# Extra output tiles between the steps of six norm chains, and weights split six units ahead instead of four

## What is computed

```
h = [meta; x]
h = h + mixer(rms_norm(h))          # differential attention (4 heads x 2) and windowed attention (8 heads), gated, merged
h = h + swiglu(rms_norm(h))         # 1024 -> 2816 -> 1024
x = rms_norm(h)
for layer in 0, 1:
    m = mixer_a(rms_norm(x)) if layer == 0 else mixer_c(rms_norm(x))
    # mixer_a: short convolution and latent attention (8 heads)
    # mixer_c: compressed, selected and windowed attention (16 heads, 4 groups), gated
    x = x + rms_norm(m)
    x = x + rms_norm(sq_relu_mlp(rms_norm(x)))     # 1024 -> 4096 -> 1024
```

## Time and profile before

| what | us |
|---|---|
| median of 3 runs | 2252.34 (2251.35 to 2252.68) |
| the profiled execution: its own time | 2250.42 |
| its span | 2248.6 |
| PE busy | 2086.2 (93%) |
| DVE busy | 1210.6 (54%) |
| ACT busy | 808.4 (36%) |
| POOL busy | 38.3 (2%) |
| mean granted clock of PE | 0.957 |

### The profile page before, as it was taken

How to read it: one execution, slowest core, us unless ns; L and a number is a source line. 1 busy time by engine, 2 the same in 40 slices (tenths; PEclk the granted TensorE clock), 3 DMA queues, 4 the chain that set the end, 5 groups by cost and what they waited for, 6 DMA issues and landing times. The chain is left out here.

```text
span 2248.6 us, 27344 instructions
## 1 busy us (share of the span) xinstructions
PE 2086.2 (93%) x10625; PEld 1011.3 (45%) x10625; DVE 1210.6 (54%) x2191; ACT 808.4 (36%) x1481; POOL 38.3 (2%) x40
## 2 busy tenths in 40 slices
PE   6978899999999988988889999979979998999996
PEld 2443454444444433435434444437446653444442
DVE  4875545546555346665376632356665536765332
ACT  3345543323233222345233321234357743332220
POOL 0100000000000002000000000000000000000000
PEclk9989999999999999989989999987989999999998
DMA  5310013324333322311213333306300011433310
GB/s 180 113 48 0 1 38 102 99 69 124 104 96 113 99 67 85 104 40 64 75 57 114 102 103 113 113 30 207 94 10 1 1 36 40 122 103 113 113 57 38
DMA packets 52185, 179.18 MB, mean 80 GB/s; under 512 B 5985, under 2 KB 9697, under 8 KB 51681
## 3 DMA queue, kind: packets, MB, share of 16 engines
q1 hardware_dynamic: 52064, 177.51, 25.7%
HBM read 174.34 MB, written 2.10 MB: 78 GB/s over the span
## 5 line engine op out<-in xcount | busy, mean ns | idle before, releaser
L1491 DVE SCALAR_TENSOR_TENSOR w_lo<-w_raw,w_hi 128x1024 f16<-128x1024 f32 x317 | 382.0, 1223 | 238.5 <-ACT w_hi L1161 238.2
L815 PE MATMUL pS<-xx,w_hi 128*128 128x512 f16 x1264 | 484.3, 383 | 19.3 <-DVE tmp L1546 14.3
L816 PE MATMUL pS<-xx,w_hi 128*128 128x512 f16 x1264 | 484.1, 383 | 0.0
L817 PE MATMUL pS<-xx,w_lo 128*128 128x512 f16 x1264 | 483.8, 383 | 0.0
L815 PE MATMUL pS<-arena,w_hi 128*128 128x512 f16 x924 | 350.7, 380 | 1.4 <-DVE arena L1506 1.4
L816 PE MATMUL pS<-arena,w_hi 128*128 128x512 f16 x924 | 350.6, 379 | 0.0
L817 PE MATMUL pS<-arena,w_lo 128*128 128x512 f16 x924 | 350.5, 379 | 0.0
L1161 ACT ACTIVATE w_hi<-w_raw 128x1024 f16<-128x1024 f32 x317 | 322.9, 1042 | 21.6 <-PE pS L838 20.9
L1170 ACT ACTIVATE arena<-src 128x512 f16<-128x512 f32 x106 | 66.7, 630 | 377.8 <-DVE src L2046 202.5
L815 PEld LDWEIGHTS pS<-xx,w_hi 128*128 128x128 f16 x1264 | 124.7, 99 | 171.5 <-DVE tmp L1546 18.3
L817 PEld LDWEIGHTS pS<-xx,w_lo 128*128 128x128 f16 x1264 | 124.7, 99 | 152.6 <-issue 6.1
(11 more groups left out here) (299 smaller groups left out, 2331.3 us busy)
## 6 DMA issues: line engine op xcount, KB each, us to landing
w_raw<-in_w SPq DMA_DIRECT2D x317, 512.0 KB, 3.6
X<-in_x SPq DMA_DIRECT2D x1, 2112.0 KB, 8.6
arena<-in_c SPq DMA_DIRECT2D x2, 1024.0 KB, 6.8
out_t<-X SPq DMA_DIRECT2D x8, 256.0 KB, 2.0
arena<-in_h SPq DMA_DIRECT2D x4, 256.0 KB, 15.0
arena<-in_h SPq DMA_DIRECT2D x2, 512.0 KB, 9.2
arena<-in_c SPq DMA_DIRECT2D x2, 256.0 KB, 4.0
arena<-arena SPq DMA_DIRECT2D x4, 128.0 KB, 2.6
```

Of the source, the lines that this page charges most:

```text
L815: pe.matmul(ps, wh, ah, start=f, stop=False)
L816: pe.matmul(ps, wh, al, start=False, stop=False)
L817: mm = pe.matmul(ps, wl, ah, start=False, stop=l)
L1491: dve.scalar_tensor_tensor(out=w_lo[:, u % WR, :], in0=w_raw[:, u % RAW, :], scalar=WS, in1=w_hi[:, u % WR, :], op0=ALU.mult, op1=ALU.subt ...
```

## The change

- `Plan` keeps two lists: `bank` (0 to 3 are `pS`, 4 is `pT[:, 0]`, 5 is `pO[:, 0]`) and `before` (the tile that had the bank last). For the stages in `SPARE` two tiles, from the number given on, get banks 4 and 5; all others take `pS`'s four in turn.
- `lead` puts the sums behind all slices, then one such tile, then the spread, then the second one. For qa's lead these are qb's tiles 0 and 1, for kvc's lead ks's, for the others the stage's own tiles 4 and 5.
- In the first block qb comes ahead of ka, on every engine and in the stream; PE waits for the eviction of qb's first two tiles ahead of ka. qb's first two units are split ahead of the norm.
- `LOOK` is 6 instead of 4. On SP three weight units go between the krp and the qrp copies.
- `ck1`'s and `cv1`'s bias columns move to `pO[:, 1]` and `pT[:, 1]`.

```diff
-LOOK = 4
+LOOK = 6
 ...
+SPARE = {"ffgu": 4, "cv": 4, "up0": 4, "up1": 4, "ks": 0, "qb": 0}
 ...
+        self.bank, self.before = [], []
+        turn, last = 0, {}
+        for s in self.order:
+            for j in range(s.n):
+                extra = j - SPARE.get(s.name, s.n)
+                b = 4 + extra if 0 <= extra < 2 else turn % 4
+                turn += b < 4
+                self.before.append(last.get(b, -1))
+                self.bank.append(b)
+                last[b] = s.o0 + j
 ...
-    [("qa", "T", 4, KD, 1), ("ka", "T", 4, KD, 1), ("va", "N", NQ, KD, 4), ("qb", "T", 4, KD, 1),
+    [("qa", "T", 4, KD, 1), ("qb", "T", 4, KD, 1), ("ka", "T", 4, KD, 1), ("va", "N", NQ, KD, 4),
 ...
+        def out_bank(o):
+
+            b = PL.bank[o]
+            return pS[:, b, :] if b < 4 else (pT, pO)[b - 4][:, 0, :]
 ...
             def bank_free(o):
 
-                if o >= 4:
-                    pe.wait_ge(evicted, o - 3)
+                if PL.before[o] >= 0:
+                    pe.wait_ge(evicted, PL.before[o] + 1)
 ...
-            def lead(s, name):
+            def lead(s, name, then):
 
                 r = PL.r[name]
                 for k in range(s.k):
-                    if k == s.k - 1:
-                        norm_sum(name, name == "x0")
                     pe.wait_ge(rhs_ready, r + k + 1)
 ...
+                norm_sum(name, name == "x0")
+                out_T(S[then], SPARE[then], xr)
                 norm_spread(name, name == "x0")
+                out_T(S[then], SPARE[then] + 1, xr)
 ...
-            lead(S["qa"], "x0")
-
-            pe.wait_ge(rs_ready, 1)
+            lead(S["qa"], "x0", "qb")
+            for j in range(2, 4):
+                out_T(S["qb"], j, xr)
+            pe.wait_ge(evicted, S["qb"].o0 + 2)
             for j in range(4):
                 out_T(S["ka"], j, xr, meta=(pT[:, 0, j * M:(j + 1) * M], xm))
             out_N(S["va"], full, meta=pT[0:M, 1, :])
-            for j in range(4):
-                out_T(S["qb"], j, xr)
             out_T(S["kb"], 0, xr, meta=(pO[:, 1, 0:M], xm))
 ...
-            lead(S["ffgu"], "x1")
-            for j in range(LEAD, 2 * KFF1):
+            lead(S["ffgu"], "x1", "ffgu")
+            for j in range(LEAD + 2, 2 * KFF1):
                 out_T(S["ffgu"], j, xr)
 ...
-            lead(S["kvc"], "p2")
-            for j in range(2):
-                out_T(S["ks"], j, xr)
+            lead(S["kvc"], "p2", "ks")
 
             pe.wait_ge(rhs_ready, PL.r["ks"])
 ...
+            split_hi(PL.out_tau[S["qb"].o0 + 1], look=0)
             act.wait_ge(basics_ready, 1)
 ...
             for j in range(4):
+                head_parts("qb", j, lambda half: q1w[:, 2 * j + half, :])
+            for j in range(4):
                 head_parts("ka", j, lambda half: k1d[:, 2 * j + half, :])
 ...
             link(dve.tensor_scalar(nlam[:, :], lam[:, 2:3], -LINIT, None, ALU.add))
+            head_parts("qb", 4, lambda j, half: q1w[:, 2 * j + half, :], lambda j, half: q1w[aux_part(half), 2 * j + half, :],
+                       lambda j, half: q2w[head_rows(half), 2 * j + half, :], 0.125)
             dve.wait_ge(zeroed, ZERO_DIFF)
             head_parts("ka", 4, lambda j, half: k1d[:, 2 * j + half, :], lambda j, half: k2d[head_rows(half), 2 * j + half, :],
 ...
+            units(ur, ur + 3)
+            ur += 3
             for j in range(2):
                 sp.wait_ge(rhs_ready, PL.r["qr"] + j + 1)
```

More of the change, by code:

```diff
@@ L167 @@
 )
-RHS = [("x0", 8), ("qa", 4), ("ka", 4), ("qb", 4), ("kb", 1), ("ya", 4), ("yb", 4), ("mrg", 8), ("x1", 8), ("ff", KFF1), ("xb", 8), ("conv", 4),
+RHS = [("x0", 8), ("qa", 4), ("qb", 4), ("ka", 4), ("kb", 1), ("ya", 4), ("yb", 4), ("mrg", 8), ("x1", 8), ("ff", KFF1), ("xb", 8), ("conv", 4),
        ("cq", 6), ("ckv", 2), ("qn", 4), ("kr", 1), ("kn", 4), ("qr", 2), ("ymla", 4), ("p1", 8), ("h0", KFF2), ("p2", 8), ("z", 4), ("pe", 1),
@@ L709, in pcol, with pe_bank @@
             return par[:, a + k:a + k + n]
+        def out_bank(o):
+            b = PL.bank[o]
+            return pS[:, b, :] if b < 4 else (pT, pO)[b - 4][:, 0, :]
+        def pe_bank(c):
+            return (pO, pT)[c][:, 1, 0:1]
         def nat_bank(c):
@@ L801, in out_T @@
                 bank_free(o)
-                ps = pS[:, o % 4, 0:n_cols]
+                ps = out_bank(o)[:, 0:n_cols]
                 for k in range(s.k):
@@ L825, in out_N @@
                     bank_free(s.o0 + t)
-                    ps = pS[:, (s.o0 + t) % 4, 0:w]
+                    ps = out_bank(s.o0 + t)[:, 0:w]
                     a = slice(t * P, (t + 1) * P)
@@ L840, in out_N, with of @@
                             mm.then_inc(mm_done, 1)
-            def lead(s, name):
+            def of(a):
+                return lambda q, k: a[q][:, k, 0:T]
+            xr = of(xa)
+            def lead(s, name, then):
                 r = PL.r[name]
                 for k in range(s.k):
-                    if k == s.k - 1:
-                        norm_sum(name, name == "x0")
                     pe.wait_ge(rhs_ready, r + k + 1)
@@ L854, in lead @@
                         wh, wl = weights(tau)
-                        ps = pS[:, o % 4, :]
+                        ps = out_bank(o)
                         pe.matmul(ps, wh, xa[0][:, k, 0:T], start=k == 0, stop=False)
@@ L1005, in attention @@
                 unit_values(run.u1 - 1)
-            def of(a):
-                return lambda q, k: a[q][:, k, 0:T]
-            xr = of(xa)
             xm = lambda q, k: xa[q][:, k, T:TM]
@@ L1044, in _ @@
             norm("x2")
-            lead(S["cv"], "xb")
-            for j in range(LEAD, 12):
+            lead(S["cv"], "xb", "cv")
+            for j in range(LEAD + 2, 12):
                 out_T(S["cv"], j, xr)
@@ L1086, in mlp @@
             def mlp(lay, p_in, h, m):
-                lead(S[f"up{lay}"], p_in)
-                for j in range(LEAD, KFF2):
+                lead(S[f"up{lay}"], p_in, f"up{lay}")
+                for j in range(LEAD + 2, KFF2):
                     out_T(S[f"up{lay}"], j, xr)
@@ L1102, in _ @@
                 bank_free(s.o0)
-                ps = pS[:, s.o0 % 4, 0:2 * NCMP].rearrange("p (a n) -> p a n", a=2)
-                bs = pO[:, c, 0:1]
+                ps = out_bank(s.o0)[:, 0:2 * NCMP].rearrange("p (a n) -> p a n", a=2)
+                bs = pe_bank(c)
                 for k in range(CL):
@@ L1129, in _ @@
             for a in range(2):
-                ps = pS[0:NCMP, s.o0 % 4, a * P:(a + 1) * P]
+                ps = out_bank(s.o0)[0:NCMP, a * P:(a + 1) * P]
                 hh, hl = (hid[q][:, 1, a * NCMP:(a + 1) * NCMP] for q in range(2))
@@ L1332, in _ @@
                 out_of(S["va"], t)
-            for j in range(4):
-                head_parts("qb", j, lambda half: q1w[:, 2 * j + half, :])
             head_parts("kb", 0, lambda half: k1w[:, half, :])
@@ L1499, in out_of @@
                 dve.wait_ge(mm_done, PL.out_ms[o])
-                return pS[:, o % 4, :]
+                return out_bank(o)
             def lo(r, dst, a, h, scale=1.0):
@@ L1828, in _ @@
                     split_lo(0, k // 2)
+            split_lo(PL.out_tau[S["qb"].o0 + 1], look=0)
             dve.wait_ge(const_loaded, 16)
@@ L1879, in _ @@
                 link(dve.tensor_scalar(vd[:, 1, t, :], vd[:, 0, t, :], nlam[:, :], None, ALU.mult))
-            head_parts("qb", 4, lambda j, half: q1w[:, 2 * j + half, :], lambda j, half: q1w[aux_part(half), 2 * j + half, :],
-                       lambda j, half: q2w[head_rows(half), 2 * j + half, :], 0.125)
             formed(S["kb"], 0)
@@ L2068, in _ @@
                 ps = out_of(S[name], 0)
-                link(dve.tensor_scalar(cst[:, c:c + 1], pO[:, c, 0:1], 1.0 / WS, None, ALU.mult))
+                link(dve.tensor_scalar(cst[:, c:c + 1], pe_bank(c), 1.0 / WS, None, ALU.mult))
                 sync()
```

## The result

The changed kernel takes 2257.49 us (median of 15 executions, 2253.40 to 2258.51); the kernel before takes 2251.98 us on the same chips (15 executions, 2250.42 to 2255.74). The ratio is 1.0019, 95% interval 1.0012 to 1.0027: 4.3 us longer (2.7 to 6.1), inside the 0.2% that the prediction called no change, though its interval excludes zero. The forecast was 3.1 us longer, a median of 2255.4. The two medians lie 5.5 us apart: 8 of the changed kernel's 15 executions took 2257.5 to 2258.5 us at a mean granted clock of 0.949 or 0.950, while 13 of the 15 of the kernel before lie under 2253. The text goes by the ratio. The profiled execution took 2255.3 us with a span of 2253.5, so 4.9 us more than the profiled one before.

A forecast was written before the change was run, and what follows sets the result against it. PE's work (busy 93% of the span), its stops at the norm chains and its low clock bound the kernel. Losses 13.6, less gains 15.8, plus clock 5.3: 3.1 us longer, 2255.4; range 2247 to 2262.

The forecast's parts named there:

- x0: First block: PE stands 14.5 us before ka instead of 7.0, waiting for DVE's eviction of qb; loss 7.2 us.
- x1, p1, p3: Leads of ffgu, up0, up1: tile 10 waits 2.7 to 3.0 us for an eviction; gains 2.8, 2.0 and 2.0 us.
- xb: Lead of cv: PE waits 2.0 us for the diagonal instead of 4.4; gain 9.0 us, before 0.8 for the clock.
- p2: Lead of kvc, with ks's tiles: PE stands 10.4 us before ck1; loss 3.8 us.
- Six units ahead: In vv, slots freed late put splits and evictions in 7.9 us instead of 5.35; loss 2.6 us, nothing gained elsewhere.
- The clock: Half clock behind the new stops: 1.5 us each at x1, p1 and p3, 0.8 at xb; cost 5.3 us.
- the clock costs more: Rival: stops at tile 10 each leave half clock for as long as kvc's 5.94 us stop did; 2262, chance 0.27.
- The wait before ka does not bind: Rival: DVE reaches qb1 by 60.8, so x0 saves the 14.5 us and the 1.4; 2239.5, chance 0.08.
- The gaps are simply filled, some 2215: Rival: at all six leads DVE catches up in time, so the gaps are filled; some 2215, chance 0.03.

The follow-up runs named there:

- e3: Changed kernel with everything around x0 as in the kernel before (qb behind va, no spare tile there); ratio 0.9987, 7.2 us under the changed kernel.
- e1: Kernel before with only the look-ahead changed, weights split six units ahead instead of four; ratio 1.0012, 2.7 us longer.
- e4: Changed kernel with sums before the last slice and spread before both tiles at five leads (xb: one tile before it); ratio 0.9919 to kernel before.
- e7: Kernel before with only xb's lead as changed, six units ahead but four in vv; ratio 0.9981, 4.3 us under the kernel before.
- e5: Changed kernel with only p2's order turned: sums before the last slice, spread, then ks's two tiles; ratio 1.0004, 3.4 us under the changed kernel.
- e10: Kernel before plus extra banks: four units ahead, x0 as before, spread before both tiles at five leads; ratio 0.9968, 7.2 us under the kernel before.
- e9: Changed kernel with x0 as before, spread first (xb: between tiles), four units ahead from vv through gt and at last attention's start; ratio 0.9880 to kernel before.
- e12: e9 with one tile in a spare bank instead of two at x1, p1 and p3; ratio 0.9875, 28.1 us under the kernel before.

## Why the prediction was right, and where it was off

The forecast (3.1 us longer, most likely no change) was right, and its terms can be checked one by one. The terms of work hold to within about 1 us each; that their sum came within 1.8 us of the profile is in part luck, since the clock moved stretches that have no edit by up to 1.1 us, both ways.

- **x0, forecast 7.2.** The stop came as forecast: 14.26 us up to 74.79 against 14.5 up to 75.3, because DVE reaches qb only behind qa and the tables. e3, which takes the reordering back, gives 7.2 us in the ratios and 6.5 in the traces, so the term is shown as 6.5 to 7.2. The 9.25 us of the table contain more: the half clock behind ka's stop lasted 5.44 us instead of 2.80, 1.3 us of it lost, and 1.4 were lost in the first attention. The trace of e1 has 2.65 us of that kind without the reordering, so they are not x0's order.
- **x1, p1, p3: forecast 2.8, 2.0, 2.0, less 1.5 each for the clock.** Net 1.3, 0.5, 0.5; measured 0.93, 0.44, 0.02. Tile 10 waited 2.5 to 2.9 us (forecast 2.7 to 3.0) on line 1566, and the clock was down for 3.3 to 3.4 us behind it. The mechanism was that of the prediction: the spread is 5.2 us late (5.99 + 2.59 - 3.40) and with it DVE and ScalarE's series of evictions, so that two tiles of head start are used up 26 us later. e4 shows it from the other side: the same tiles, behind the spread, remove the stop.
- **xb, forecast 9.0 less 0.8.** Measured 8.94, and 8.96 in e7. The diagonal's wait was 1.81 us (forecast 2.0), and the product that met the fills grew from 1.36 to 2.17 us, which left tile 10 0.40 us short. The clock did not fall behind it: the window above has PEclk 1.00, so the 0.8 was not paid. The reason for the low price was a poor one, though. The 2.45 us stop of x0 that "left its next matmuls fast" was followed by only 1.44 us of PE's work and then by the stop ahead of ka, and the clock fell 0.49 us into that one (granted 1.00 from 41.42 to 43.35, 0.50 from 43.35 to 50.17); the 2.49 us stop of x1 left its next matmuls fast too, for 1.30 us, and then half clock for 3.41. The Trainium skill (GPSIMD Engine Reference, section 1, Specifications) would have DVE's splits held up beside the fills; in the changed kernel too they took 1.22 us there, against four diagonals that took 5.63, so its half on instructions with two SBUF inputs is not borne out.
- **p2, forecast 3.8.** ck1 waited 10.35 us (forecast 10.4) and starts 2.64 us later than before (1524.43 against 1521.79), where p2's chain had been 1.14 us early: 3.8. e5 gives 3.4 us back.
- **Six units ahead, forecast 2.6.** The last attention starts 4.97 us later than before (1639.55 against 1634.58), ck1 2.64, so 2.3 lie between them; in e1's trace it is 1.6, and e1's ratio of 2.7 (0.7 to 4.7) is too wide to tell them apart. The step was right on where, a little high on how much, and wrong in a sentence beside it: "PE waited for a split once, at the start, so nothing is gained". e10 shows what the deeper look-ahead is for. At x1 and xb the extra tiles reach PE before their weights are split at four units; e9, six ahead, is 19.8 us faster. e9 and e10 differ in one more thing, the tile ahead of xb's spread, which needs the six: 11.3 us of the difference lie at xb in the traces, 8.2 at x1, p1 and p3, where the order is the same. In the changed kernel no such wait was ever seen, so I had priced the cost of the look-ahead and not its use.
- **The clock, forecast 5.3.** 1.7 each at x1, p1 and p3 (3.3 to 3.4 us at half clock), 0 at xb: 5.1. What I had not priced is the clock in stretches that the change does not touch: +0.55 from x2 to xb, +1.08 from mc to p3 (the half clock at the start of p3's lead lasted 5.6 us instead of 3.4), -1.1 in the last attention.

The rows of the table add to 4.89 us and the terms to 3.1. The 1.8 between them are 2.05 at x0, 0.9 at x1, p1 and p3 together and 1.0 in stretches without an edit, less 0.74 at xb and 1.43 from p2 to mc: each no larger than what the clock moved elsewhere; which of them are the clock's is shown only for x0 and for the stretches without an edit. The rival "the clock costs more" asked for 6 us at half clock behind each tile 10; there were 3.4. "The wait before ka does not bind" fell with 14.26 us. "The gaps are simply filled, some 2215" fell for this change; the kernel that puts the spread first came to 2224.99, and nearer to it than to the kernel before.

What stays open is why the half clock behind one and the same stop lasts 2.8 and 2.9 us in two profiles of the kernel before and 5.9 in e1 and e10, though the instructions of e10 up to there are the same. That executions of one kernel differ by 5 us along with their clock is shown; which of the stretches carry it in the unprofiled ones is not.

## What to carry to other kernels

When a stop on a chain is filled with moved work, put the filler behind the instruction that the other engines wait for, not ahead of it: here a tile of 5.2 us ahead of the spread made every eviction 5.2 us late and gave the gain back 26 us later, and the same tile behind it was worth 5 us per lead. A filler needs all of its inputs early, a free bank and split weights both; the banks in the right order gave 7.2 us, the look-ahead alone -2.7, both together 28 (with the tile ahead of xb's spread, which needs both). A wait on a counter should name the one event that the next instruction needs: one number too many cost 4.3 us ahead of ka.

## What the runs showed of the hardware

- **The clock's answer to a stop is not a function of the stop.** Half clock (1.2 GHz) followed a stop of 3.60 us for 2.54 us in one kernel and 5.94 in another, at the same place. A stop of 14.26 us left 5.44, one of 10.0 left 5.54, stops of 2.5 to 2.9 us left 3.3 to 3.4, and one of 1.81 left none. So a half-clock term can be priced only to within some 1.7 us for each stop, half the distance from 2.54 to 5.94. The Trainium skill (TensorE: Matmul & The Clock Gate, Part 1) says that how many matmuls run at the low clock varies from run to run of one kernel; the three groups of executions of the kernel before, at 0.957, 0.954 and 0.952, agree.
- **The clock moves stretches that no edit touches.** The last attention, the same 1400 matmuls, took 243.69 us in the kernel before, 242.55 in the changed one and 245.26 in e5; PE's busy time in it was 228.65, 227.55 and 231.57 us, at granted clocks of 0.96, 0.96 and 0.94. A difference of 2.7 us between two profiles can lie there alone.
- **A profiled execution stands for one group only.** Both profiles of the kernel before are of its shortest group, 5 us under its longest, which is more than the change was worth.
- **Filling small stops pays one and a half times.** At x1 a stop of 3.60 us cost 3.60 and half of the 3.34 at half clock: 5.3 us; the table has 5.45 for e12.
